# Strassen products for two blocks of the SwiGLU feed-forwards of a two-layer trunk

## The chip, the core and the metric

The kernel runs on one core of a Trainium2 chip, as one program. The metric is the device time in microseconds (us) of one execution, taken as the median of several runs. All arithmetic is float32; TensorE gets its precision from operands split in two (below).

## The reference, cut to what matters

Two layers. Each layer is a SwiGLU feed-forward (FFN) with half weight, a token mixer, and a second such FFN. There are 256 tokens of width 1024; the hidden width of an FFN is 2816. The four FFNs are what the change touches:

```
def _rms_norm(x, g):
    y = x32 * lax.rsqrt(jnp.mean(x32 * x32, axis=-1, keepdims=True) + EPS)
    return (y * g.astype(jnp.float32)).astype(x.dtype)

def _swiglu(h, w_gate, w_up, w_down):
    return (jax.nn.silu(h @ w_gate) * (h @ w_up)) @ w_down

x = x + 0.5 * _swiglu(_rms_norm(x, ffn1_norm[l]), ffn1_w_gate[l], ffn1_w_up[l], ffn1_w_down[l])
...   # mixer: input projection, causal convolution, latent attention, gates, output projection
x = x + 0.5 * _swiglu(_rms_norm(x, ffn2_norm[l]), ffn2_w_gate[l], ffn2_w_up[l], ffn2_w_down[l])
```

Here h is [256, 1024], w_gate and w_up are [1024, 2816], w_down is [2816, 1024].

## The kernel before, in words

**Products.** Every operand of TensorE is kept as a rounded part (whi, hThi, gThi) and the remainder (wlo, hTlo, gTlo). One float32 product is three matmuls (`products`, L663 to L665): hi by hi, hi by lo, lo by hi.

**Units.** Weights pass through the core in units of [128 partitions, 2048] float32, 1 MB each. SyncE (SP) loads a unit by two DMAs of 512 KB into `raw` (3 buffers); ScalarE (ACT) rounds it into `whi` (`split`, L1123); VectorE (DVE) subtracts to get `wlo` (`split`, L1517). whi and wlo have RING = 6 slots, so a unit can be made only after TensorE (PE) has released the unit six places before it. Each raw buffer comes free when the wlo of the unit three places before is done. All of these are one numbered sequence, and each engine's program is a list written out by hand in which the order of the work is fixed.

**The FFN.** The 2816 features go in 11 chunks c of 256 columns. A chunk has two units G0, G1 (gate and up columns of the upper and of the lower half of the 1024 rows) and one unit D (256 rows of w_down). For a tile of 128 tokens (t = 0, 1), `gate_up(c, t)` sums 8 x 3 matmuls of 512 columns into one PSUM bank; `down(c, t)` does 4 x 3 matmuls of 512 columns. So a chunk is 72 matmuls of 512 columns, and PE runs gate_up(c, 0), gate_up(c, 1), down(c-2, 0), down(c-2, 1) (`pair`). Between them ACT takes the silu (L1216), DVE multiplies (`mul`, L1623), ACT separates the halves of the words (`split_planes`, L1225), SP turns them by a transposing DMA (`plane_turn`), DVE joins them (`join`, L1636), ACT rounds (`round_joined`, L1233) and DVE subtracts (`rest_joined`, L1522). The chunks in the middle run in hardware loops on each engine, two to a turn.

**Around it.** At the start of an FFN two units are ready; the ring fills up while PE works on the first chunks. GpSimd (POOL) does one `root` (L531) for each RMS norm, and once in each layer a chain of some 70 small operations for the rotary angles (L549 to L588), which in the program stands right after the root of the first FFN; ACT waits for its end at the start of the mixer, and the roots of the mixer's norm stand behind it in POOL's program. In the mixer POOL also subtracts 12 units in each layer (L645).

Of the kernel before, what the change touches and what calls it, by code (L numbers as in the profile page):

```python
# [26 lines left out]
P = 128  # L27
# [29 lines left out]
U_FFN = 3 * NCH  # L57
# [4 lines left out]
assert U_LAYER % RING == 0 and U_LAYER % RAW == 0  # L62
# [32 lines left out]
def unit_gu(f, c, h):  # L95

    if isinstance(c, int) and c < 2:
        return UB[f] + 2 * c + h
    return c * 3 + (UB[f] - 2 + h)

def unit_down(f, c):

    if isinstance(c, int) and c >= NCH - 2:
        return UB[f] + U_FFN - NCH + c
    return c * 3 + (UB[f] + 6)
# [21 lines left out]
def trunk(nc, a):  # L128
    with ExitStack() as ctx:
# [16 lines left out]
        gain = sb("gain", [P, D])  # L146
        gates = sb("gates", [P, TT, 2 * D])
        ktok = sb("ktok", [P, TT, H, QK])
        vtok = sb("vtok", [P, TT, H, VD])
        cu = sb("cu", [P, CT, W - 1 + SEQ])  # L150
        cacc = sb("cacc", [P, CT, SEQ])
        qkT = sb("qkT", [P, 2, 2 * SEQ])
        pT = sb("pT", [P, 2, 3 * P])
        bias = sb("bias", [P, C])
# [14 lines left out]

        ss = small[:, 0:2]  # L170
# [12 lines left out]
        g_turned = vtok[:, 0, :, :].rearrange("p h d -> p (h d)")  # L183
# [3 lines left out]
        spare = ktok.rearrange("p t h d -> p (t h d)")  # L187
        block_words = (qkT[:, 0, :], spare[:, 0:512])
        block_turned = (turned, spare[:, 512:1024].bitcast(U16).rearrange("p (j r) -> p j r", r=P))
        block_out = (g_turned, cacc[:, 0:2, :].rearrange("p c n -> p (c n)"))  # L190
        sgate = gates[:, 0, 0:TT * FC].rearrange("p (t f) -> p t f", t=TT)
        gu = gates[:, 1, 0:TT * FC].rearrange("p (t f) -> p t f", t=TT)
# [115 lines left out]
        stored = sem("stored")  # L308

# [6 lines left out]
        def unit_waits(eng, l, u):  # L316

            eng.wait_ge(wlo_ready, l * U_LAYER + u + (RAW + 1))
# [4 lines left out]

        def per_ffn(l, f, c, t):
            return l * (4 * NCH) + c * TT + (2 * NCH * f + t + 1)

# [24 lines left out]
        def gu_bank(c, t):  # L351

            return bank[:, (6 if isinstance(c, int) and c == 1 else 4) + t, :]

        def slot(u, n):
            return u % n
# [10 lines left out]

        block = ctx.enter_context(nc.Block())

        @block.sync
        def _(sp):
            def place(l, u, u0, pairs):

                sp.wait_ge(wlo_ready, l * U_LAYER + u + 1)
                for dst, src in pairs:
                    sp.dma_start(dst, src).then_inc(raw_landed[slot(u0, RAW)], 16)

            def gate_up(l, f, c, c0, h):
                u0 = unit_gu(f, c0, h)  # L380
                dst = raw[:, slot(u0, RAW), 0:2048].rearrange("p (k g n) -> p k g n", k=4, g=2)
                rows = slice(4 * h * P, 4 * (h + 1) * P)
                cols = bass.ds(c * FC, FC)
                place(l, unit_gu(f, c, h), u0, [
# [1618 lines left out]
```

## Time and profile before

| | |
|---|---|
| median of 3 runs | 1047.74 us (1047.26 to 1047.82) |
| the profiled execution, first to last instruction (span) | 1045.7 us |
| outside the span (median less span) | 2.0 us |
| PE busy | 1040.6 us |
| DVE busy | 687.1 us (66%) |
| ACT busy | 593.7 us (57%) |
| POOL busy | 248.9 us (24%) |
| DMA | 208.81 MB, queue of SP 63.6% of 16 engines' span |

A page of the profile gives for each engine its busy time, the granted clock of TensorE, the chain of work that ended last, and groups of instructions by source line. Matmuls overlap in the records: one of 512 columns is shown as 0.39 us, and what it costs is the distance from one start to the next. An engine's idle time is put down to whatever released it.

### The profile page before, as it was taken

To read this page: it belongs to the slowest core of one execution; us is meant where nothing else is said; L and a number is where in the kernel's file an instruction comes from. 1 tells how busy PE (TensorE), PEld (TensorE's weight loads), DVE (VectorE), ACT (ScalarE), POOL (GpSimd) and SP (SyncE) were. 2 spreads that over 40 slices of the span, in tenths; PEclk is the share of its full clock that TensorE was granted. 3 is DMA by queue.
4 is the path that set the end of the run, shared out by engine and by line. 5 is a ranking of instruction groups with operands and counts; after the bars stand their busy time and mean duration, and the time that the engine had idled before them with its cause. 6 is when DMAs were issued, how large, how long until landed. Compare 5 with 4: busy or idle time off the path is not lost.

```text
span 1045.7 us, 13767 instructions
## 1 busy us (share of the span) xinstructions
PE 1040.6 (100%) x5001; PEld 872.2 (83%) x5001; DVE 687.1 (66%) x911; ACT 593.7 (57%) x792; POOL 248.9 (24%) x258
## 2 busy tenths in 40 slices
PE   9999999999999999999999999999999999999998
PEld 6888888998888888888888888889988888888887
DVE  6755655698976766555576555656999677656551
ACT  6754544576874665445466454536778557645440
POOL 2960000148850000000048300002588300000000
PEclk9999999999999999999999999999999999999999
DMA  8977666455644696675569667565366366976641
GB/s 280 310 237 234 186 211 200 143 200 172 210 163 125 206 313 188 206 232 196 153 191 282 216 206 228 184 199 172 122 212 224 118 191 222 261 221 186 207 139 41
DMA packets 191555, 208.81 MB, mean 200 GB/s; under 512 B 64112, under 2 KB 162704, under 8 KB 191504
## 3 DMA queue, kind: packets, MB, share of 16 engines
q1 hardware_dynamic: 190288, 206.03, 63.6%
q10 hardware_dynamic: 1216, 2.11, 0.7%
q8 instruction: 31, 0.51, 0.2%
q14 instruction: 20, 0.16, 0.1%
HBM read 192.90 MB, written 1.05 MB: 185 GB/s over the span
## 4 chain that ended last, share of the span: by engine, by line
PE 98%; ACT 1%; DVE 1%; issue 0%; POOL 0%; ACTq 0%
PE bank L663 31%; PE bank L665 31%; PE bank L664 31%; PE bank L744 1%; PE bank L905 1%; PE bank L914 1%; PE bank L935 1%; PE bank L670 1%; PE bank L702 0%; PE bank L913 0%; PE bank L937 0%; DVE htok L1563 0%; DVE x L1611 0%; ACT htok L1132 0%; PE bank L923 0%; PE bank L963 0%
## 5 line engine op out<-in xcount | busy, mean ns | idle before, releaser
L1517 DVE TENSOR_TENSOR wlo<-raw,whi 128x2048 fp32r<-128x2048 f32 (+2 forms) x152 | 347.4, 2290 | 82.6 <-ACT whi L1123 81.5
L663 PE MATMUL bank<-whi,hThi 128*128 128x512 f32 (+1 forms) x976 | 378.4, 388 | 0.0
L665 PE MATMUL bank<-whi,hTlo 128*128 128x512 f32 (+1 forms) x976 | 373.7, 383 | 0.0
L664 PE MATMUL bank<-wlo,hThi 128*128 128x512 f32 (+1 forms) x976 | 373.6, 383 | 0.0
L1123 ACT ACTIVATE whi<-raw 128x2048 fp32r<-128x2048 f32 (+2 forms) x176 | 335.3, 1910 | 16.8 <-DMA raw<-in_ffn_w_up 7.3
L665 PEld LDWEIGHTS bank<-whi,hTlo 128*128 128x128 f32 x976 | 183.3, 188 | 35.7
L663 PEld LDWEIGHTS bank<-whi,hThi 128*128 128x128 f32 x976 | 183.4, 188 | 35.1 <-issue 0.3
L664 PEld LDWEIGHTS bank<-wlo,hThi 128*128 128x128 f32 x976 | 183.4, 188 | 34.8
L1216 ACT ACTIVATE gates<-bank,small 128x256 f32<-128x256 f32 x88 | 41.8, 475 | 263.5 <-PE bank L665 262.8
L663 PE MATMUL bank<-whi,gThi 128*128 128x512 f32 (+1 forms) x416 | 162.2, 390 | 0.0
L664 PE MATMUL bank<-wlo,gThi 128*128 128x512 f32 (+1 forms) x416 | 161.1, 387 | 0.0
L665 PE MATMUL bank<-whi,gTlo 128*128 128x512 f32 (+1 forms) x416 | 161.1, 387 | 0.0
L531 POOL TENSOR_TENSOR small<-small,expo 128x1 f32<-128x1 f32 (+3 forms) x20 | 24.2, 1214 | 566.3 <-DVE small L1556 529.5
L1623 DVE SCALAR_TENSOR_TENSOR gates<-bank,small,gates 128x256 f32<-128x256 f32 x88 | 42.4, 483 | 168.1 <-ACT gates L1216 168.0
L645 POOL TENSOR_TENSOR wlo<-raw,whi 128x2048 fp32r<-128x2048 f32 x24 | 110.2, 4612 | 21.9 <-ACT whi L1123 21.9
L1717 DVE SCALAR_TENSOR_TENSOR bank<-cu,vec,bank 128x256 f32<-128x256 f32 x240 | 98.1, 479 | 0.2
L665 PEld LDWEIGHTS bank<-whi,gTlo 128*128 128x128 f32 x416 | 78.1, 188 | 16.0
L663 PEld LDWEIGHTS bank<-whi,gThi 128*128 128x128 f32 x416 | 78.1, 188 | 15.8 <-issue 0.4
L664 PEld LDWEIGHTS bank<-wlo,gThi 128*128 128x128 f32 x416 | 78.2, 188 | 15.5
L1225 ACT ACTIVATE qkT<-gates 128x512 uint16<-128x512 uint16 x80 | 49.5, 620 | 0.0
L549 POOL TENSOR_TENSOR small<-expo 128x1 f32<-128x1 f32 x72 | 36.5, 507 | 5.9
L663 PE MATMUL bank<-hThi,whi 128*128 128x256 f32 x128 | 36.4, 284 | 0.0
(177 smaller groups left out, 823.6 us busy)
## 6 DMA issues: line engine op xcount, KB each, us to landing
raw<-in_ffn_w_down SPq DMA_DIRECT2D x88, 512.0 KB, 4.2
raw<-in_ffn_w_gate SPq DMA_DIRECT2D x84, 512.0 KB, 4.3
raw<-in_ffn_w_up SPq DMA_DIRECT2D x84, 512.0 KB, 5.4
raw<-in_w_in SPq DMA_DIRECT2D x48, 512.0 KB, 4.8
raw<-in_w_out SPq DMA_DIRECT2D x16, 512.0 KB, 4.4
raw<-in_w_in SPq DMA_DIRECT2D x8, 544.0 KB, 4.5
raw<-in_w_mla_out SPq DMA_DIRECT2D x8, 512.0 KB, 3.9
raw<-in_w_conv_out SPq DMA_DIRECT2D x8, 512.0 KB, 4.7
```

The lines of the kernel that those rows point to most:

```text
L531: return nc.gpsimd.tensor_tensor(out, in_, expo[:, :].to_broadcast([P, out.shape[-1]]), ALU.pow)
L549: nc.gpsimd.tensor_tensor(small[:, 95:96], expo[:, :], expo[:, :], ALU.mult)
L645: nc.gpsimd.tensor_tensor(wlo[:, slot(u, RING), 0:n], raw[:, slot(u, RAW), 0:n], whi[:, slot(u, RING), 0:n].bitcast(F32), ALU.subtract).th ...
L663: nc.tensor.matmul(out, lh, rh, start=start, stop=False, skip_group_check=skip)
L664: nc.tensor.matmul(out, lh, rl, start=False, stop=False, skip_group_check=skip)
L665: return nc.tensor.matmul(out, ll, rh, start=False, stop=stop, skip_group_check=skip)
L1123: nc.scalar.activation(whi[:, slot(u0, RING), 0:USED[u0]], raw[:, slot(u0, RAW), 0:USED[u0]], ACT.Copy).then_inc(whi_ready, 1)
L1216: nc.scalar.activation(sgate[:, t, :], gu_bank(c, t)[:, 0:FC], ACT.Silu, scale=rs[:, t:t + 1]).then_inc(silu_ready, 1)
L1225: nc.scalar.activation(planes[:, :, :, t, :], words, ACT.Copy).then_inc(planes_ready, 1)
L1517: nc.vector.tensor_tensor(wlo[:, slot(u0, RING), 0:n], raw[:, slot(u0, RAW), 0:n], whi[:, slot(u0, RING), 0:n].bitcast(F32), ALU.subtract) ...
L1623: nc.vector.scalar_tensor_tensor(out=gu[:, t, :], in0=gu_bank(c, t)[:, FC:2 * FC], scalar=rs[:, t:t + 1], in1=sgate[:, t, :], op0=ALU.mult ...
L1717: ins = nc.vector.scalar_tensor_tensor(out=o, in0=i, scalar=w, in1=o, op0=ALU.mult, op1=ALU.add)
```

## The change

Chunks 3 and 4, and chunks 7 and 8 (features 768 to 1279 and 1792 to 2303), are computed as two blocks of 512 features. A block's input product has 2 x 2 x 2 quarters: token tiles t, halves of the 1024 rows, gate or up columns. Before, that is 8 quarter products of 4 x 3 matmuls. The change does 7, by Strassen's scheme in Winograd's form:

- On the weights, four sums of quarters (B11 is the upper quarter of gate, B21 its lower one, B22 the lower quarter of up): T1 = B11 + upper quarter of up, T2 = T1 + B22, T3 = both quarters of up, T4 = T2 + B21; the signs are in the sums of the tokens. The new list of units for a block is B11, T1, D, T2, B22, B21, T3, T4, D: nine units, where the two chunks had six. T1 and T2 are added by DVE into `chain[0]`; T3 and T4 are made by DMAs of GpSimd that add the lower quarter from HBM into `chain[1]` and `chain[0]` (`add_rows`, two DMAs of 512 KB each). chain[0] lies in `htok`, chain[1] in the memory of ktok and pT.
- On the tokens, once for an FFN: h is put together again (`whole_rows`), four sums of quarters (`mixed_rows`), rounded (`mixed_round`) and subtracted (`mixed_rest`) into new tiles sThi, sTlo. These share their memory with gain, bias, vtok and cu.
- On the results: PE leaves some products in the same bank and goes on adding to them; ACT copies the bank in between (`keep`, four a block), DVE adds or subtracts the copies (`up_first`, `gate_first`, `up_second`, `gate_second`), ACT's silu and DVE's multiply then work on 512 columns at once.

All engines' loops are written out, in a new order; an FFN has 39 units instead of 33. POOL's `sums` (the four `add_rows` of an FFN) stands in its program after the roots of that FFN's norm, and in the first FFN of a layer before the rotary angles. The memset of cu moves into the mixer. The core of the diff:

```
-U_FFN = 3 * NCH
+BLK = (3, 7)
+CW = 2 * FC
+PRODUCTS = ("B11", "T1", "D0", "T2", "B22", "B21", "T3", "T4", "D1")
...
             for l in range(DEPTH):
                 norm(l, 0)
+                sums(l, 0)
...
+            def add_rows(l, f, c, name):
+                done = per_block(l, f, c)
+                if name == "T3":
+                    pool.wait_ge(chain_landed[1], done * 32)
+                    pool.wait_ge(sum_ready["T1"], done)
+                    dst, src = chain[1], quarter_of(wu[f], l, c, 1)
+                if name == "T4":
+                    pool.wait_ge(wlo_ready, l * U_LAYER + unit_block(f, c, "T2") + 1)
+                    dst, src = chain[0], quarter_of(wg[f], l, c, 1)
+                dst = dst.rearrange("p (k n) -> p k n", k=4)
+                for k in (0, 2):
+                    nc.gpsimd.dma_start(dst[:, k:k + 2, :], src[:, k:k + 2, :],
+                                        accum_op=ALU.add).then_inc(sum_ready[name], 16)
...
+                    block_product(c, "B11", 4, plain_T(0, 0))
...
+                    block_product(c, "T1", 5, mixed_T(1, 1))
+                    down(c - 2, 0)
+                    down(c - 2, 1)
+                    pe.wait_ge(kept_ready, (done - 1) * 4 + 1)
+                    block_product(c, "T2", 4, mixed_T(0, 0), start=False)
+                    pe.wait_ge(kept_ready, (done - 1) * 4 + 2)
+                    block_product(c, "B22", 5, mixed_T(1, 0), start=False)
+                    pe.wait_ge(gu_ready, per_gu(l, f, at6, 0))
+                    block_product(c, "B21", 6, plain_T(1, 0))
+                    pe.wait_ge(kept_ready, (done - 1) * 4 + 3)
+                    block_product(c, "T3", 4, mixed_T(0, 1), start=False)
+                    pe.wait_ge(gu_ready, per_gu(l, f, at6, 1))
+                    block_product(c, "T4", 7, plain_T(1, 1))
+                    down(c - 1, 0)
+                    down(c - 1, 1)
...
                 first()
-                pair(2, 2)
-                pair(3, 3)
-                with pe.Fori(0, (NCH - 5) // 2) as i:
-                    pair(i * 2 + 4, 4)
-                    pair(i * 2 + 5, 5)
+                pair(2)
+                strassen(3)
+                pair(5)
+                pair(6)
+                strassen(7)
+                pair(9)
                 last()
```

DVE's list of one FFN, up to the end of the first block (the second block's follows the same pattern):

```
+                    gate_split(1, 0)
+                    gate_split(1, 1)
                     mul(0, 0)
                     norm_scale(l, 2 * f, 1)
+                whole_rows()
+                if (l, f) != (0, 0):
+                    mul(0, 1)
+                mixed_rows()
+                gate_split(2, 0)
+                gate_split(2, 1)
+                down_split(0)
+                join(0)
+                mul(1, 0)
+                mul(1, 1)
+                of_chain(3, "B11")
+                add_T1(3)
+                rest_joined(0)
+                mixed_rest()
+                mul(2, 0)
+                mul(2, 1)
+                of_chain(3, "T1")
+                join(1)
+                add_T2(3)
+                down_split(1)
+                rest_joined(1)
+                of_chain(3, "T2")
+                lower(3, "B22")
+                lower(3, "B21")
+                of_chain(3, "T3")
+                join(2)
+                up_first(3)
+                rest_joined(2)
+                of_chain(3, "T4")
+                down_split(2)
+                up_second(3)
+                gate_first(3)
+                block_mul(3, 0)
+                gate_second(3)
+                gate_split(5, 0)
+                block_mul(3, 1)
+                gate_split(5, 1)
```

ACT's list around the third to fifth product of the first block:

```
+                sum_of(3, "T2")
+                keep(3, 0, "B11")
+                lower(3, "B22")
+                lower(3, "B21")
+                split_planes(2, 1)
+                keep(3, 1, "T1")
+                sum_of(3, "T3")
+                keep(3, 2, "T2")
+                round_joined(2)
+                sum_of(3, "T4")
+                down_split(2)
+                keep(3, 3, "T3")
```

## Rows read from the trace of the kernel before

**Rows 1.** The page: span, busy time of the engines, TensorE's granted clock.

```profile
span 1045.7 us, 13767 instructions
...
PE 1040.6 (100%) x5001; PEld 872.2 (83%) x5001; DVE 687.1 (66%) x911; ACT 593.7 (57%) x792; POOL 248.9 (24%) x258
...
PEclk9999999999999999999999999999999999999999
```

**Rows 2.** The page: the chain that ended last, share of the span by engine.

```profile
PE 98%; ACT 1%; DVE 1%; issue 0%; POOL 0%; ACTq 0%
```

**Rows 3.** Timeline of PE in an FFN: start us, us, what.

```profile
60.03 0.39 PE L664 MATMUL bank<-wlo,gThi 128*128 128x512 f32 x1
...
65.25 0.39 PE L663 MATMUL bank<-whi,hThi 128*128 128x512 f32 x1
```

**Rows 4.** Groups by line and shape: busy us, mean ns | idle before, releaser.

```profile
L1517 DVE TENSOR_TENSOR wlo<-raw,whi 128x2048 fp32r<-128x2048 f32 x146 | 334.4, 2294 | 79.6 <-ACT whi L1123 78.5
L1123 ACT ACTIVATE whi<-raw 128x2048 fp32r<-128x2048 f32 x170 | 324.5, 1913 | 16.1 <-DMA raw<-in_ffn_w_up 7.3 <-DMA raw<-in_w_in 4.6 <-DMA raw<-in_ffn_w_down 1.6
...
L1636 DVE COPY vtok<-qkT 128x1024 uint16<-128x1024 uint16 x40 | 30.2, 755 | 0.0
L1522 DVE TENSOR_TENSOR gTlo<-vtok,gThi 128x512 fp32r<-128x512 f32 x40 | 27.4, 686 | 3.3 <-ACT gThi L1233 3.3
L1233 ACT ACTIVATE gThi<-vtok 128x512 fp32r<-128x512 f32 x40 | 24.9, 622 | 18.1 <-DVE vtok L1636 17.6 <-PE bank L665 0.5
```

**Rows 5.** A stretch of one chunk: length, busy (x) of PE, PEld, DVE, ACT, POOL, PEclk, DMA share, GB/s.

```profile
395.00:411.30 16.30, 16.30 (x74) 13.50 (x73) 9.12 (x7) 7.92 (x8) 0.00 (x0) 1.00 0.68 210
```

**Rows 6.** Timeline at the start of the second FFN: PE, ACT, DVE.

```profile
345.07 0.39 PE L663 MATMUL bank<-whi,hThi 128*128 128x512 f32 x1
...
347.79 1.03 PE L702 MATMUL bank<-ident,x 128*128 128x128 f32 x8
...
350.44 1.97 ACT L1123 ACTIVATE whi<-raw 128x2048 fp32r<-128x2048 f32 x1
352.25 0.52 ACT L1216 ACTIVATE gates<-bank,small 128x256 f32<-128x256 f32 x1
...
352.44 2.29 DVE L1517 TENSOR_TENSOR wlo<-raw,whi 128x2048 fp32r<-128x2048 f32 x1 [0.67 <-ACT whi L1123]
354.65 0.48 DVE L1623 SCALAR_TENSOR_TENSOR gates<-bank,small,gates 128x256 f32<-128x256 f32 x1
```

**Rows 7.** The first FFN: DVE before the unit G0 of chunk 2, and PE.

```profile
24.73 0.87 DVE L1623 SCALAR_TENSOR_TENSOR gates<-bank,small,gates 128x256 f32<-128x256 f32 x2
25.57 2.29 DVE L1517 TENSOR_TENSOR wlo<-raw,whi 128x2048 fp32r<-128x2048 f32 x1
...
32.62 0.38 PE bank L663
```

**Rows 8.** Loads of units: KB and median us to landing, then all of SP's.

```profile
raw<-in_ffn_w_up SPq DMA_DIRECT2D x84, 512.0 KB, 5.4
...
DMA to landing us min/median/max: 3.1/4.7/9.5
```

**Rows 9.** Rotary angles on POOL, the root behind them; DVE beside them; stretch of each layer's.

```profile
22.29 0.19 POOL L554 CAST small<-posi 128x2 f32<-128x2 int32 x1
...
36.27 0.20 POOL L549 TENSOR_TENSOR small<-expo 128x1 f32<-128x1 f32 x1
36.54 2.44 POOL L564 TENSOR_SCALAR ang<-ang 128x32 f32<-128x32 f32 x1
...
179.89 0.57 POOL L531 TENSOR_TENSOR small<-small,expo 128x1 f32<-128x1 f32 x1 [107.03 <-DVE small L1556]
...
36.53 2.29 DVE L1517 TENSOR_TENSOR wlo<-raw,whi 128x2048 fp32r<-128x2048 f32 x1 [0.29 <-ACT whi L1123]
...
22.30:72.90 50.60, 50.60 (x224) 41.72 (x223) 35.91 (x29) 32.39 (x34) 45.53 (x88) 1.00 1.00 293
536.70:587.30 50.60, 50.60 (x225) 41.92 (x224) 34.05 (x25) 29.86 (x31) 45.33 (x88) 1.00 0.94 283
```

More of the change, by code:

```diff
@@ L61 @@
 UM = U_FFN
-assert U_LAYER % RING == 0 and U_LAYER % RAW == 0
+assert U_LAYER % RING == 0
+LOADED = [u for f in range(2) for u in range(UB[f], UB[f] + U_FFN)
+          if FFN_UNITS[u - UB[f]][0] in ("G0", "G1", "D", "B22", "B21")] + list(range(UM, UM + U_MIX))
+LOADED.sort()
+R_LAYER = len(LOADED)
+UPPER = (1, 5, 9)
+SUM = {"T1": 1, "T2": 1, "T3": 32, "T4": 32}
+PLAIN = [c for c in range(NCH) if not any(b <= c < b + 2 for b in BLK)]
 M_PR, M_C01, M_UQ, M_UKV, M_C23, M_G, M_MLA, M_CO, M_WO = 0, 2, 4, 5, 6, 8, 16, 18, 20
@@ new lines, in ffn @@
+                down(l, f, 4)
+                turn(4)
+                chain_load(l, f, 7, 1)
+                down(l, f, 5)
+                turn(5)
+                lower_load(l, f, 7, "B22")
+                lower_load(l, f, 7, "B21")
+                turn(6)
+                down(l, f, 6)
+                gate_up(l, f, 9, 0)
+                gate_up(l, f, 9, 1)
+                down(l, f, 7)
+                gate_up(l, f, 10, 0)
+                turn(7)
+                gate_up(l, f, 10, 1)
@@ L808, in turn, with down @@
                     ins.then_inc(gtr, 1)
-                def down(c, c0, t, last=False, between=None):
+                def down(c, t, last=False, between=None):
                     pe.wait_ge(glo, per_ffn(l, f, c, t))
@@ new lines, in ffn @@
+                split_planes(5, 1)
+                round_joined(4)
+                first_of(7, "B11")
+                silu(6, 0)
+                sum_of(7, "T1")
+                silu(6, 1)
+                down_split(5)
+                round_joined(5)
+                split_planes(6, 0)
+                split_planes(6, 1)
+                sum_of(7, "T2")
+                round_joined(6)
+                lower(7, "B22")
+                keep(7, 0, "B11")
+                lower(7, "B21")
+                keep(7, 1, "T1")
@@ new lines, in ffn @@
+                gate_split(5, 0)
+                block_mul(3, 1)
+                gate_split(5, 1)
+                join(3)
+                down_split(3)
+                rest_joined(3)
+                gate_split(6, 0)
+                join(4)
+                mul(5, 0)
+                gate_split(6, 1)
+                mul(5, 1)
+                down_split(4)
+                of_chain(7, "B11")
+                rest_joined(4)
+                add_T1(7)
+                mul(6, 0)
+                join(5)
@@ new lines, in ffn @@
+                of_chain(7, "T1")
+                mul(6, 1)
+                add_T2(7)
+                down_split(5)
+                rest_joined(5)
+                of_chain(7, "T2")
+                join(6)
+                lower(7, "B22")
+                rest_joined(6)
+                lower(7, "B21")
+                of_chain(7, "T3")
+                of_chain(7, "T4")
+                down_split(6)
+                up_first(7)
+                gate_split(9, 0)
+                up_second(7)
```

593 lines of the change are left out of this document (442 added, 151 removed).

## The prediction

> **What bounds the kernel now.** I read the page first: of a span of 1045.7 us PE is busy 1040.6, at the full granted clock (2.4 GHz) in every slice [rows 1]. DVE and ACT are at 66% and 57% [rows 1]. The chain that ended last is PE to 98% [rows 2]. So the bound is the number of matmuls, and a matmul taken away is worth its whole distance to the next, provided that nothing else becomes late. In the timeline of an FFN the reader should look at starts, not at durations: from 60.03 to 65.25 there are 23 matmuls of 512 columns, 0.227 us each [rows 3]. A chunk of 72 is 16.3 us. In one such stretch DVE is busy 9.1 us and ACT 7.9, with the DMA engines at 0.68 [rows 5]: the room that the added work has to fit in.
>
> **What is removed.** Two chunks take 96 matmuls for gate and up; a block takes 7 x 12 = 84. That is 12 less for each block, 96 for eight blocks (two in each of four FFNs): 96 x 0.227 = 21.8 us, all of it on the path. This term I trust most. 1047.7 - 21.8 = 1025.9 is the floor; I see nothing by which it could go lower, since PE had no gaps that the written-out loops could close.
>
> **What is added on PE.** No matmul. More waits, at each product instead of at each second one; each costs only if what is waited for is late. So the rest is a question of lateness, for DVE, ACT, the adding DMAs and POOL.
>
> **DVE and ACT, in sum.** For a block: nine units instead of six (3 more remainders of 2.29 us, 3 more roundings of 1.91 [rows 4]), two sums T1 and T2 (an operation of three operands of the same size as a remainder, so 2.29 each), four sums of results and two multiplies of 512 columns (0.69 each, as L1522 [rows 4]), four copies on ACT (0.62 each, as L1233 [rows 4]). DVE in a block: 9 x 2.29 + 2 x 2.29 + 6 x 0.69 + two joins (0.76) and two rests (0.69) = 32.2 us; PE takes 132 x 0.227 = 29.9 us. So DVE is slower than PE inside a block, and it fits only by what was made ahead in the six slots and by the light chunks between. For an FFN: whole_rows, mixed_rows and mixed_rest add 2.29 + 4 x 0.69 + 2.29 = 7.3 us, at its start, where the ring is only two units deep.
>
> **DVE, step by step in the first block.** Take PE's times in units of 12 matmuls, 2.72 us: in the second FFN they start at 345.07, and eight transposes at 347.79 put in some 0.85 [rows 6], so product number k starts at 345.9 + 2.72 k. G0 of chunk 2 is due at k = 8 (367.7), D0 at k = 12 (378.6), T4 at k = 22 (405.8), G0 and G1 of chunk 5 at k = 25, 26 (413.9, 416.6). Queued remainders follow each other at 2.21 us and roundings at 1.81, small DVE operations at 0.4 to 0.65 (354.65 less 352.44, 352.25 less 350.44 [rows 6]). Walking DVE's list from 352.44: two remainders to 356.9; mul, scale, whole_rows, mul to 360.0; mixed_rows with its waits for its own steps to 362.7; G0 of chunk 2 ready at 364.9, slack 2.8; G1 3.0; D0 ready 369.6; join, two muls, B11 373.2, T1's sum 375.4, rest_joined(0) 376.0, slack 2.6 to D0's product; mixed_rest 378.2; mul(2,1) waits for PE (378.6) and silu to 379.5; T1 381.7, slack 5; join, T2's sum 384.5, D1 386.7, rest_joined(1) 387.3, slack 2.1; T2 389.5; B22, B21, T3 to 396.1. Then `up_first` waits at the head of DVE's queue until PE has done B22 (k = 20, 400.3), and rest_joined(2), T4, D2 and the units of chunk 5 stand behind it: T4 403.8, slack 2.0; D2 406.0, slack 2.5; after the four sums and a multiply G0 of chunk 5 at 412.1, slack 1.8, and G1 at 414.9, slack 1.7. So no product is late, but everything has only some 2 us, and a list of 40 steps has handoffs of about 0.1 us that I left out. The second block begins with a full ring, and the same walk gives 3.5 us and more. I put 0.2 us a block for handoffs, 1.6 us in all; bounds 0 and, if each first block loses what its slack falls short of a 2 us error, 4 x 2 = 8.
>
> **The first FFN** has no slack to begin with. DVE is done with its two muls at 25.57 and then made G0 of chunk 2, which PE took at 32.62 [rows 7]. Now whole_rows and mixed_rows (2.2 + 2.7) come before it: 25.6 + 4.9 + 2.3 = 32.8. That is 2.9 us less slack than in the other FFNs, and so at rest_joined(1) about 0.8 us late. Cost 1.0 us; bounds 0 and 3, since the DMA engines are at 1.00 in that stretch [rows 9].
>
> **The adding DMAs.** The trace of before has none. T3's can start at 375.4 and is wanted by ACT at some 392, so it is covered. T4's may be issued only when T2's remainder is done (389.5), since it changes chain[0] in place; ACT would take it at 398.6. Behind it on ACT stand D2's rounding, `keep` of T3 and the units of chunk 5. With DVE's 1 us of reserve there and the slack of 1.7, PE loses nothing while the two DMAs land within L = 11.8 us of T2's remainder. In the second block T2' can't be ready before PE has ended gate_up(6, 1) (k = 35, 441.1), then silu, mul, sum, D5, rest and remainder, 449.2; T4' is due at k = 45 (468.3), less 1.9 and 2.3: L may be 14.9. A plain load of half a unit lands in 4.7 us in the median, 5.4 for w_up, at most 9.5 [rows 8]. Lower bound of L: 4.7. Upper bound: an add reads two sources, twice the slowest, 19. The nearest is twice the 5.4, 10.8, with an issue of two DMAs ahead of it: about 11.5, just inside. Price of L: 4 (L - 11.8) + 4 (L - 14.9), so nothing at 11.5 and 45 us at 19. A page of the Trainium skill speaks to this: "Collectives: The Full Stack", "The bandwidth ceiling", says that a reducing transfer is half as fast as a copy because the add needs two source reads. With the fixed 2.0 us plus bytes / 436e3 of "DMA: Bandwidth & Descriptors", "Anatomy of one DMA", an estimate from the two is 2.0 + 2 x 2.4 = 6.8 us for 1 MB, and the cost of T4 would be 0. No run here shows either so far. Of bytes: 2 MB more for each block, 16 to 208.8 MB; at a share of 0.68 this has room outside the first 60 us.
>
> **POOL's queue.** In the first FFN of each layer the rotary angles now stand behind `sums`, and so behind the wait for T2' of the second block. They take 50.6 us in both layers [rows 9] (ends 72.9 and 587.3). In the first FFN product k starts at 32.6 - 8 x 2.72 = 10.9 plus 2.72 k; T2' is ready 8.3 us after k = 35, at 114.4, the issues take some 2 us, the angles end at 167. The root behind them ran at 179.89 [rows 9], and is due 5.4 us earlier now (two blocks less), at 174.5: 7.5 us to spare, so cost 0. ACT's wait for the angles comes later still. What they could lose: POOL's small operations grow from 0.2 to 2.44 us when a remainder of DVE runs (36.54 beside 36.53 [rows 9]). DVE's load beside them was 35.9 and 34.1 of 50.6 us [rows 9]; in the new place I count 13 remainders and some small ones, 34 of 53, the same.
>
> **Sum.** 1047.7 - 21.8 + 1.6 + 1.0 = 1028.5 us. The profiled execution would be at 1026.5 by its own span (2.0 outside it).
>
> **The rivals.**
> 1. *The adding DMAs are late* (L = 12 to 16): PE waits before T4 of the first block of each FFN, then of the second as well. For it: they compete with D2's and chunk 5's loads, the slowest plain landing is 9.5, and POOL makes two of them. Against: the DMA share of 0.68. At L = 14, 4 x 2.2 = 9 us: 1037. Chance 0.15.
> 2. *The angles are late.* If the denser DVE stretches them by a quarter, to 63 us, they end at 180, 5 us behind the root's due time in two layers, which PE has some 2 us of cover for: 6 us, up to 12 if more: 1035 to 1041. By the page "SBUF — State Buffer", "Who interferes with whom", a DVE operation with two inputs in SBUF contends with GpSimd's reads; by that rule the row pair at 36.5 agrees, and the stretch grows with DVE's count in that time. Chance 0.10.
> 3. *DVE is late in the first block* by handoffs that my walk lacks, 1 to 3 us in each FFN: 1031 to 1038. Chance 0.09.
> 4. *Slower than before.* The one mechanism is again the landing of T4, now as a rate: if an add moves float32 so slowly that 8 L - 106.8 exceeds the gain of 19.2 (what is left after the two terms above), so from L = 15.8 us on, less than 67 GB/s for the megabyte. At the bound of 19 it is 1028.5 + 45 = 1074. Chance 0.06.
> 5. *It doesn't save what it says*, because products with waits at each 12 matmuls leave gaps of about 0.2 us in PE: 7 waits x 8 x 0.2 = 11 us, 1040. Against: PE waited as often in the mixer with no gap in its busy time. Chance 0.03.
>
> **How the numbers follow.** The forecast (every lateness under about 4 us in sum, 1026 to 1031) has 0.57. Rivals 1, 2, 3 and 5 together 0.37, nearly all faster still, since they give 1031 to 1044. Rival 4 has 0.06. The range: down to 1025.4, the floor less the spread of the runs; up to 1039, which takes in rivals 3, most of 1 and half of 2; above it I leave some 0.13. A measurement can tell about 0.2% (2.1 us) from no change: faster means under 1045.6, same 1045.6 to 1049.8. From the cases: faster 0.91, same 0.03, slower 0.06.
>
> **What the profile after would show.** 96 fewer matmuls of 512 columns, 4905 in all, and PE's sum of gaps under 9 us. If the forecast holds, PE has no idle time named after whi or wlo outside the first 60 us; the adds land within 12 us; the last rotary operation ends by 170 and by 680. Wrong if: PE idles before T4 (k = 22) in each FFN, released by DVE after ACT after a DMA (rivals 1 and 4); idles at the start of the mixer, with POOL's root behind the angles (rival 2); idles a little before many products of the first block with DVE never idle (rival 3); or shows small gaps at every wait (rival 5).

## The result: slower by 4%

The changed kernel takes 1089.87 us (median of 4 runs, 1082.84 to 1093.68), the kernel before, beside it, 1047.50 (1046.66 to 1047.82). The ratio is 1.040, 95% interval 1.0383 to 1.0417. The forecast was 1028.5 us, in a range of 1025.4 to 1039, with 0.06 for slower: wrong in size and in sign. The profiled execution has a span of 1087.0 us and took 1088.85.

The page of the changed kernel, to be held against [rows 1]:

```profile
span 1087.0 us, 13335 instructions
...
PE 1037.7 (95%) x4905; PEld 864.5 (80%) x4905; DVE 811.7 (75%) x992; ACT 661.2 (61%) x836; POOL 288.7 (27%) x290
...
PEclk9989998999999998999999899999999999989999
...
q0 software_dynamic: 8704, 16.78, 9.6%
```

The 96 matmuls are gone (4905), yet PE is busy for 1037.7 us, only 2.9 less than before. It is idle for 49.3 us, where it was idle for 5.1. And its granted clock is not full in every slice any more (the line PEclk, in tenths). The last line of the view is the queue of GpSimd's adding DMAs: packets, MB, and their share of the 16 DMA engines' time. PE's list of waits (what it waited for; us in total, times, longest) names two places:

```profile
PE bank L854 <- DVE wlo L1880: 33.3, 9, 6.0
PE bank L1053 <- DVE gates L1989: 10.5, 4, 4.3
```

The first is the product T4, once in each of the eight blocks (in order of time 5.98, 2.53, 4.94, 1.41, 4.68, 4.69, 5.58 and 3.32 us) and once for 0.2 us, before G0 of chunk 2 in the first FFN. The second is the last chunk's turn at the end of each FFN (4.29, 2.68, 2.56, 1.01), which the prediction did not look at.

With the 96 x 0.227 = 21.8 us that were to go, the span adds up: 1045.7 - 21.8, plus 44.2 more idle time (49.3 - 5.1), plus 18.9 of PE's busy time over 1040.6 - 21.8 = 1018.8, gives 1087.0.

**T4's add, in one block.** Timeline of the changed kernel, first block of the second FFN: start us, us, what (and the idle time before it):

```profile
400.20 2.28 DVE L1880 TENSOR_TENSOR wlo<-htok,whi 128x2048 fp32r<-128x2048 f32 x1
...
402.85 1.21 POOL L717 DMA_DIRECT2D htok<-in_ffn_w_gate  x1 [5.83 <-DVE wlo L1880]
409.06 1.52 POOL L717 DMA_DIRECT2D htok<-in_ffn_w_gate  x1 [5.01 <-issue]
...
419.16 1.91 ACT L1369 ACTIVATE whi<-htok 128x2048 fp32r<-128x2048 f32 x1 [7.56 <-DMA htok<-in_ffn_w_gate]
...
421.11 2.29 DVE L1880 TENSOR_TENSOR wlo<-htok,whi 128x2048 fp32r<-128x2048 f32 x1 [6.61 <-ACT whi L1369]
...
423.55 0.76 PE L854 MATMUL bank<-whi,hThi 128*128 128x512 f32 x1 [4.94 <-DVE wlo L1880]
424.11 0.63 PE L855 MATMUL bank<-wlo,hThi 128*128 128x512 f32 x1
...
428.37 0.58 PE L856 MATMUL bank<-whi,hTlo 128*128 128x512 f32 x1
428.79 0.39 PE L854 MATMUL bank<-whi,gThi 128*128 128x512 f32 x1
```

T2's remainder is done at 402.48 and POOL issues the first add 0.37 us later. The second add leaves only at 409.06, 6.2 us behind the first, though POOL has nothing else to do ("issue" as the releaser: the profile shows nothing it waited for). ACT gets the sum at 419.16. So L, counted from the end of T2's remainder to ACT's start, is 16.7 us, and PE is 4.94 us late. Four stretches of the same time show the DMA engines before the landing and TensorE after its wait (length; busy of PE, PEld, DVE, ACT, POOL; granted clock; DMA share; GB/s):

```profile
402.90:409.00 6.10, 6.10 (x29) 5.05 (x28) 6.10 (x3) 3.72 (x4) 1.16 (x1) 1.00 0.95 211
409.10:419.10 10.00, 9.51 (x42) 7.53 (x41) 2.05 (x3) 1.12 (x2) 1.48 (x1) 1.00 0.95 259
...
423.50:428.80 5.30, 5.25 (x13) 4.13 (x14) 4.05 (x4) 3.56 (x3) 0.00 (x0) 0.50 0.83 271
428.80:434.00 5.20, 5.20 (x24) 4.31 (x23) 5.01 (x4) 3.29 (x5) 0.00 (x0) 1.00 0.49 155
```

The DMA share is 0.95, not the 0.68 of [rows 5]. And after the wait the granted clock is 0.50, the lower of the two levels (1.2 GHz): behind the first of them the matmuls of T4 stand 0.427 us apart, where the following ones are 0.23 apart. A wait of 4.94 us thus costs about another 12 x 0.2 = 2.4 us, which is booked as busy. Over the whole trace 72 distances are so wide, in eight runs of 7 to 11 (14 single ones in the mixers are not counted: the kernel before has them too). The eight runs stand behind or soon after the waits of 2.56, 3.32, 4.29, 4.68, 4.69, 4.94, 5.58 and 5.98 us; behind the waits of 1.01, 1.41, 2.53 and 2.68 us there are none. That is 72 x 0.2 = 14.4 of the 18.9 us. The length of a wait does not decide it alone: in the kernel of experiment 2 eight wide distances follow a wait of 2.03 us, and none follow one of 3.19 us.

**The end of an FFN.** SP, ACT, DVE and PE at the end of the second FFN:

```profile
516.85 0.38 SPq L485 DMA_DIRECT2D raw<-in_ffn_w_gate  x1
...
517.88 1.63 SPq L534 DMA_TRANSPOSE qkT<-qkT  x1
...
510.95 1.15 ACT L1522 ACTIVATE qkT<-gates 128x512 uint16<-128x512 uint16 x2 [0.88 <-DVE gates L1989]
512.60 3.71 ACT L1369 ACTIVATE whi<-raw 128x2048 fp32r<-128x2048 f32 x2
...
514.53 6.76 DVE L1880 TENSOR_TENSOR wlo<-raw,whi 128x2048 fp32r<-128x2048 f32 x3 [1.04 <-ACT whi L1369]
523.14 0.74 DVE L2004 COPY gates<-qkT 128x1024 uint16<-128x1024 uint16 x1 [1.85 <-DMA qkT<-qkT]
...
525.84 0.44 PE L1053 MATMUL bank<-ident,gates 128*128 128x128 f32 x2 [2.68 <-DVE gates L1989]
```

Chunk 9's planes are ready at 512.1, but its transpose is issued at 517.88: in SP's program it stands behind the load of the next unit, and that one waits until a raw buffer is free, at 516.8 (the first of DVE's three remainders from 514.53). The join at 523.14, the rounding, the multiply of chunk 10 and PE follow from there.

SP's order is the same in the kernel before, where it cost nothing. There the load had left at 492.23 and the planes were ready at 495.84, so that the transpose left at 495.86:

```profile
492.23 0.38 SPq L377 DMA_DIRECT2D raw<-in_ffn_w_gate  x1
...
495.86 1.23 SPq L402 DMA_TRANSPOSE qkT<-qkT  x1
...
495.22 0.62 ACT L1225 ACTIVATE qkT<-gates 128x512 uint16<-128x512 uint16 x1
```

What the change moved is the moment at which the raw buffer comes free. The load waits for the remainder of D8. ACT's list before had the rounding of D8 ahead of chunk 9's planes; the new list has it behind them and behind chunk 8's rounding (`split_planes(9, 1)`, `round_joined(8)`, `down_split(8)`), where it starts at 512.60 without a wait. That this place in ACT's list alone frees the buffer late is read from the lists and the trace; no run moved it back.

### The profile page after: what moved, and what is told of

Read it like the earlier page. It is cut to its first block and busy times, and to the rows that moved or that the text cites. A ratio compares the mean times of both kernels' runs of the same rounds, so it can differ in the third digit from the quotient of the medians.

```text
span 1087.0 us, 13335 instructions
## 1 busy us (share of the span) xinstructions
PE 1037.7 (95%) x4905; PEld 864.5 (80%) x4905; DVE 811.7 (75%) x992; ACT 661.2 (61%) x836; POOL 288.7 (27%) x290
## 3 DMA queue, kind: packets, MB, share of 16 engines
q0 software_dynamic: 8704, 16.78, 9.6%
## 5 line engine op out<-in xcount | busy, mean ns | idle before, releaser
L854 PE MATMUL bank<-whi,hThi 128*128 128x512 f32 (+1 forms) x816 | 321.8, 394 | 33.3 <-DVE wlo L1880 33.3
L1880 DVE TENSOR_TENSOR wlo<-raw,whi 128x2048 fp32r<-128x2048 f32 (+2 forms) x136 | 308.1, 2284 | 32.0 <-ACT whi L1369 31.9
L856 PE MATMUL bank<-whi,hTlo 128*128 128x512 f32 (+1 forms) x816 | 316.1, 387 | 0.0
L855 PE MATMUL bank<-wlo,hThi 128*128 128x512 f32 (+1 forms) x816 | 316.1, 387 | 0.0
L1369 ACT ACTIVATE whi<-raw 128x2048 fp32r<-128x2048 f32 (+2 forms) x160 | 301.5, 1907 | 14.9 <-DMA raw<-in_w_in 4.4
L854 PEld LDWEIGHTS bank<-whi,hThi 128*128 128x128 f32 x816 | 156.1, 191 | 66.1 <-issue 36.8
L1880 DVE TENSOR_TENSOR wlo<-htok,whi 128x2048 fp32r<-128x2048 f32 x32 | 73.2, 2288 | 62.4 <-ACT whi L1369 62.4
L1369 ACT ACTIVATE whi<-htok 128x2048 fp32r<-128x2048 f32 x32 | 61.3, 1915 | 87.3 <-DMA htok<-in_ffn_w_gate 54.0
L717 POOL DMA_DIRECT2D heads<-in_ffn_w_up x16 | 19.8, 1239 | 311.5 <-DVE htok L2028 270.8
L2246 DVE SCALAR_TENSOR_TENSOR bank<-shared,vec,bank 128x256 f32<-128x256 f32 x240 | 98.1, 479 | 0.2
L854 PEld LDWEIGHTS bank<-whi,gThi 128*128 128x128 f32 x416 | 79.6, 191 | 16.9 <-issue 0.7
L1522 ACT ACTIVATE qkT<-gates 128x512 uint16<-128x512 uint16 x80 | 48.3, 623 | 42.3 <-DMA qkT<-qkT 17.4
L2004 DVE COPY gates<-qkT 128x1024 uint16<-128x1024 uint16 x40 | 30.2, 754 | 38.6 <-DMA qkT<-qkT 38.6
```

Of the source, the lines that this page charges most:

```text
L717: nc.gpsimd.dma_start(dst[:, k:k + 2, :], src[:, k:k + 2, :], accum_op=ALU.add).then_inc(sum_ready[name], 16)
L854: nc.tensor.matmul(out, lh, rh, start=start, stop=False, skip_group_check=skip)
L855: nc.tensor.matmul(out, lh, rl, start=False, stop=False, skip_group_check=skip)
L856: return nc.tensor.matmul(out, ll, rh, start=False, stop=stop, skip_group_check=skip)
L1369: nc.scalar.activation(whi[:, slot(u, RING), 0:USED[u]], src, ACT.Copy).then_inc(whi_ready, 1)
L1522: nc.scalar.activation(planes[:, :, :, t, :], words, ACT.Copy).then_inc(planes_ready, 1)
```

## The experiments

Kernel N below is the kernel of experiment N. Ratios are to the kernel before, run beside it.

**1. T4's add left out.** The T4 adds and ACT's wait for them go; everything else stays. T4's product then takes T2's sum, so the values are not the right ones.

```
-                add_rows(l, f, 3, "T4")
...
-                add_rows(l, f, 7, "T4")
...
+                    if name != "T4":
+                        act.wait_ge(sum_ready[name], per_block(l, f, c) * SUM[name])
```

> This kernel leaves out the adding DMAs of T4 (8 of 16 pairs) and ACT's wait for them, so the T4 product uses T2's sum; all else stands. Theory A (the landing of T4's add, 14 to 17 us behind T2's remainder, makes PE wait, and the clock's fall after each wait comes with it): the eight waits of PE before the T4 product (33.3 us in all) go, about 2.5 us of half clock behind each go too, so 1089.9 - 33 - 8 x 2.4 = some 1038 if the waits at turn(10, 0) stay (10.5 us), some 1026 to 1030 if they go as well. Rival B (DVE itself is late in the first block, the add only comes last): PE waits 2 to 4 us at other products of the same blocks, 1045 or more.

Measured: 1039.11 us (1038.29 to 1039.93), ratio 0.992 (0.9903 to 0.9943). That is 1 us from the 1038 expected for the case that the waits at the FFN's end stay. PE's waits inside the blocks are gone; those at the FFN's end are 7.4 us. So T4's add is worth some 50 us, and the Strassen order alone is faster than before.

**2. Plain copies in place of the adds.** The same queue, bytes, places and waits, without the accumulation (the sums then hold other values):

```
-                    nc.gpsimd.dma_start(dst[:, k:k + 2, :], src[:, k:k + 2, :],
-                                        accum_op=ALU.add).then_inc(sum_ready[name], 16)
+                    nc.gpsimd.dma_start(dst[:, k:k + 2, :], src[:, k:k + 2, :]).then_inc(sum_ready[name], 16)
```

> This kernel makes the four GpSimd DMAs of an FFN plain copies (no add), with the same waits, so the chains hold other values. If reading two sources makes the adds slow (the rule that a reducing transfer goes at half the rate): the second DMA of a pair is issued some 3 us behind the first instead of 6.2, and the time falls to about 1050. If GpSimd's way of issuing is what is slow, whatever the operation: the distance stays at 5 to 6.2 us and the time stays over 1075.

Measured: 1037.61 us (1036.39 to 1038.82), ratio 0.991 (0.9889 to 0.9929): even less than the 1050 expected. From its page (span, PE, the queue) and POOL's timeline:

```profile
span 1034.6 us, 13335 instructions
...
PE 1021.5 (99%) x4905; PEld 854.8 (83%) x4905; DVE 811.5 (78%) x992; ACT 658.6 (64%) x836; POOL 288.4 (28%) x290
...
q0 software_dynamic: 4608, 16.78, 4.9%
...
388.90 1.45 POOL L717 DMA_DIRECT2D htok<-in_ffn_w_gate  x2 [11.80 <-DVE wlo L1879]
```

Both copies are issued within 1.45 us, and no product waits. The same 16.78 MB take 4.9% of the engines' time in 4608 packets, as adds 9.6% of a longer span in 8704. So neither the bytes nor POOL's place is what is slow; the accumulation is, in two ways: about twice the engine time, and the second DMA held back. The whole difference to the changed kernel is 1087.0 - 1034.6 = 52.4 us: 33.1 of waits before T4, 3.0 at the FFN's ends, and 16.2 of PE's busy time, for the same 4905 matmuls. Kernel 2 has 8 wide distances, behind one wait at an FFN's end, where the changed kernel has 72: 64 x 0.2 = 12.8 of the 16.2 us is the lower clock.

The doubling agrees with the Trainium skill, "Collectives: The Full Stack", "The bandwidth ceiling: the fold count and why AG ≠ RS ≠ AR", where the reducing step of a collective needs two source reads; this case has no collective, so the agreement is in the factor alone. The prediction's estimate of 6.8 us for 1 MB, with the formula of the Trainium skill, "DMA: Bandwidth & Descriptors", "Anatomy of one DMA", is not borne out: 16.7 us here, for two DMAs one after the other beside the loads of another queue.

**3. Four adds of 256 KB in place of two of 512 KB.**

```
-                for k in (0, 2):
-                    nc.gpsimd.dma_start(dst[:, k:k + 2, :], src[:, k:k + 2, :],
+                for k in range(4):
+                    nc.gpsimd.dma_start(dst[:, k:k + 1, :], src[:, k:k + 1, :],
```

Measured: 1107.41 us (1104.57 to 1109.22), ratio 1.057 (1.0551 to 1.0592): worse. That two or three pieces go out at once was as expected, the gain was not. POOL's timeline, same block:

```profile
396.16 2.82 POOL L717 DMA_DIRECT2D heads<-in_ffn_w_up  x3 [16.75 <-DVE htok L2028]
404.48 0.87 POOL L717 DMA_DIRECT2D heads<-in_ffn_w_up  x1 [5.49 <-issue]
409.54 2.66 POOL L717 DMA_DIRECT2D htok<-in_ffn_w_gate  x3 [4.20 <-DVE wlo L1880]
422.54 0.87 POOL L717 DMA_DIRECT2D htok<-in_ffn_w_gate  x1 [10.35 <-issue]
```

Three small adds go out in a row; the fourth waits 5.5 us, for T4 10.35. So it is not that every add waits for the one before: in this block three of 256 KB go out, or one of 512 KB. The last piece starts later than the second half did, 13.0 us behind the first piece against 6.2, and L is 19.8 us (409.23 to 429.02) in place of 16.7; PE's waits for remainders grow to 50.7 us. That the room is one for packets fits the numbers but was not tried by itself: the queue's packets divided by its DMAs are 272 for an add of 512 KB, 144 for one of 256 KB and 144 for a copy of 512 KB, so what goes out together has 3 x 144 = 432, 272 or 2 x 144 = 288 packets, and two adds of 512 KB would have 544.

**4. The transpose ahead of the next load.** Only SP's order at the two places where a new stage begins:

```
                     else:
-                        gate_up(l, f, 0, 0)
                         if f == 0:
                             plane_turn(l - 1, 1, NCH - 2)
+                        gate_up(l, f, 0, 0)
...
-                    if h == 1:
+                    if h == 0:
                         plane_turn(l, 0, NCH - 2)
```

> Only the order of two steps in SP's list: the transposing DMA of chunk 9 ahead of the load of the unit behind the FFN, which waits for D8's remainder. Theory: in the changed kernel that wait holds the transposing DMA back by some 5 us (issued 517.9, planes ready some 512), and PE waits at turn(10, 0) for 10.5 us in all; so 8 to 11 us less, 1079 to 1082, with the waits before T4 as they were. Rival: the join is late since DVE is behind from the late T4s, and the order doesn't matter: 1088 to 1090.

Measured: 1076.69 us (1075.16 to 1080.60), ratio 1.029 (1.0254 to 1.0316). PE's waits at the turn fall from 10.5 to 1.4 us, its busy time from 1037.7 to 1034.8, while T4's waits are 34.4 instead of 33.3: 10.7 us between the spans, 13 between the medians, where 8 to 11 were expected. With T4's waits unchanged, the second place costs on its own; experiments 6 and 7 show 9.4 us for the same edit where T4's waits are gone.

**5. T3 and T4 added by GpSimd** from the raw buffer of B22 and B21, which are loaded anyway:

```
-                    nc.gpsimd.dma_start(dst[:, k:k + 2, :], src[:, k:k + 2, :],
-                                        accum_op=ALU.add).then_inc(sum_ready[name], 16)
+                nc.gpsimd.tensor_tensor(dst, dst, raw[:, raw_slot(l, u), 0:2048],
+                                        ALU.add).then_inc(sum_ready[name], 1)
```

SP also waits for these sums before it fills the two raw buffers again, here and wherever DVE makes a sum (experiments 6, 7 and 9 to 11), so that a buffer is held longer.

> T3 and T4 are added by GpSimd's TENSOR_TENSOR from the raw buffers of B22 and B21, which are loaded anyway, in place of the adding DMAs: 4.6 us each by the 24 remainders that GpSimd makes in the mixer. T4 is ready 5 us behind T2's remainder, where DMAs took 14 to 17. Theory A: PE's waits before T4 go, 1026 to 1040, faster than before. Rival B (DVE's list in the first block is the limit): 1045 or more. If GpSimd's reads beside DVE's slow DVE (two inputs from SBUF each), DVE's remainders would be shown longer than 2.29 us.

Measured: 1076.59 us (1075.32 to 1080.70), ratio 1.028 (1.0260 to 1.0294). The time misses the 1026 to 1040 expected: the waits moved to another product. POOL and DVE in its timeline:

```profile
388.28 4.95 POOL L719 TENSOR_TENSOR heads<-heads,raw 128x2048 f32<-128x2048 f32 x1 [16.31 <-DVE htok L2030]
406.29 11.63 POOL L719 TENSOR_TENSOR htok<-htok,raw 128x2048 f32<-128x2048 f32 x1 [13.06 <-DVE wlo L1882]
...
388.67 6.72 DVE L1889 TENSOR_TENSOR sTlo<-gates,sThi 128x2048 fp32r<-128x2048 f32 x1
...
406.13 4.48 DVE L1882 TENSOR_TENSOR wlo<-raw,whi 128x2048 fp32r<-128x2048 f32 x2
410.54 2.28 DVE L1882 TENSOR_TENSOR wlo<-heads,whi 128x2048 fp32r<-128x2048 f32 x1
```

A subtraction of DVE that takes 2.29 us elsewhere takes 6.72 beside POOL's add; POOL's next add takes 11.63 us while three remainders of DVE run through it undisturbed. The two do not share, they take turns, and whoever comes second waits. PE now waits for `rest_joined`'s output gTlo (17.6 us, eight times, 2.5 or less) where it waited for T4, and still 10.3 us at the FFN's ends. This agrees with the Trainium skill, "SBUF — State Buffer", "Who interferes with whom", which calls the port pair that the two share an exclusive lock; what the trace adds is that POOL's operation can be held over several of DVE's.

**6. T4 added by DVE**, from the raw buffer of B21; T3 stays an adding DMA:

```
+                def add_T4(c):
+                    split_of(c, "T2")
+                    add(c, "T4", lower_raw(c, "B21"))
...
                 join(2)
+                add_T4(3)
                 up_first(3)
...
                 lower(7, "B21")
+                add_T4(7)
                 of_chain(7, "T3")
```

> T4's sum by DVE from B21's raw buffer, T3's still by adding DMAs. DVE gets 2.2 us more in each block, of which it idled 2.75 us ahead of up_first in the first. Theory A (T4's landing): as without T4's add at all, 1036 to 1042, the waits at turn(10, 0) left. Rival B (DVE's list has no room): PE waits 1 to 3 us at D2 or G0 of chunk 5 in each FFN, 1045 to 1055.

Measured: 1042.51 us (1042.02 to 1044.77), ratio 0.996 (0.9947 to 0.9973). No product waits for T4 (waits for a remainder 0.8 us in all); the FFN's ends cost 8.7 us. It is just over the 1036 to 1042 expected.

**7. Both: T4 by DVE, and the transpose ahead of the load.**

> Both edits: T4 by DVE and the transposing DMA of chunk 9 first. If the two causes are all that is wrong: 1026 to 1031, the floor of 1025.9 nearly reached, and faster than before by some 1.8%. If there is a third: over 1034.

Measured: 1033.15 us (1030.69 to 1033.61), ratio 0.986 (0.9843 to 0.9879). PE is busy 1020.8 us of a span of 1031.0, with a granted clock of 1.0. The time lies between my two cases, 1026 to 1031 and over 1034: the two causes are nearly all, and 3.7 us of waits stay at the turn.

**8. T4's product after D's**, so that the add has 24 more matmuls (5.4 us) to land; the adds stay, the lists of ACT and DVE follow.

```
-                    pe.wait_ge(gu_ready, per_gu(l, f, at6, 1))
-                    block_product(c, "T4", 7, plain_T(1, 1))
                     down(c - 1, 0)
                     down(c - 1, 1)
+                    pe.wait_ge(gu_ready, per_gu(l, f, at6, 1))
+                    block_product(c, "T4", 7, plain_T(1, 1))
```

> The adding DMAs stay, but T4's product comes behind the 24 matmuls of D, 5.4 us later (with the lists of ACT and DVE to match). The add lands 14 to 17 us behind T2's remainder; PE then needs it by some 17 us in the first block. Theory A: waits before T4 shrink from 33 us in all to 0 to 8, 1045 to 1060 with the waits at turn(10, 0). If each microsecond of a wait costs only itself: near 1060. If the clock's fall behind a wait goes with it: below 1050.

Measured: 1085.35 us (1084.43 to 1090.79), ratio 1.038 (1.0342 to 1.0413), far over what I expected. PE's waits:

```profile
PE bank L1053 <- DVE gates L1989: 22.4, 4, 6.3
PE bank L854 <- DVE wlo L1880: 16.7, 16, 2.1
PE bank L854 <- DVE gTlo L1887: 3.4, 5, 0.8
```

The waits for remainders are halved and spread over 16 places, but the turn at the FFN's end now costs 22.4 us instead of 10.5. The adds leave as far apart as before (400.46 and 406.84). ACT still stands idle for T4's landing in each of the eight blocks, 45.6 us in all where it was 53.8 in the changed kernel, so room on PE did not free the engines that wait for the DMA in order. As I read it, what stands behind that wait in the lists of ACT and DVE comes late at another place. SP's order has a part in it that is open: at the end of the second FFN the transpose leaves 5.8 us behind its planes (508.24 to 514.02), as in the changed kernel, and this kernel was not run with the order of experiment 4.

**9. As 7, with silu and multiply of chunk 10 ahead of chunk 9's rounding and join.**

```
-                round_joined(c - 1)
                 silu(c, 0)
+                round_joined(c - 1)
...
+                mul(c, 0)
                 join(c - 1)
                 rest_joined(c - 1)
-                mul(c, 0)
```

> As the kernel with T4 by DVE and the transposing DMA of chunk 9 first, and at the end of an FFN silu(10, 0) and mul(10, 0) come ahead of chunk 9's rounding and join, since PE wants them first. If what is left of PE's waits at turn(10, 0) (3.7 us in four FFNs, with some 2 us of lower clock behind them) comes from that order: 1033.2 less 4 to 6, 1027 to 1029. If it comes from DVE being behind in its whole list: no change, 1033.

Measured: 1031.44 us (1030.24 to 1033.84), ratio 0.985 (0.9831 to 0.9868). The wait at the turn is gone, but 4.3 us of a new one stand one step on, before the product with chunk 9's remainder (gTlo). It can't be told from kernel 7 (1033.15), and misses the 1027 to 1029 I expected. It has the lowest median of the study, 1.5% under the kernel before.

**10. T3 by DVE, T4 by the adding DMA**: the mirror of kernel 6, to see whether T3's adds in POOL's queue are what holds T4's up.

```
+                def add_T3(c):
+                    dve.wait_ge(sum_ready["T1"], per_block(l, f, c))
+                    add(c, "T3", lower_raw(c, "B22"))
...
                 lower(3, "B22")
+                add_T3(3)
                 lower(3, "B21")
```

> The opposite choice: T3 by DVE, T4 still by the two adding DMAs, all else as in the changed kernel. If T4's lateness comes partly from T3's pair still being in the DMA queues and in GpSimd's: its add lands 2 to 3 us earlier, and the waits before T4 fall from 33 to 15 us or so, 1065 to 1075. If T4's own two DMAs, one behind the other, are all of it: 1085 to 1095, with DVE's 2.2 us more in each block.

Measured: 1077.81 us (1077.06 to 1078.57), ratio 1.029 (1.0271 to 1.0312). POOL, ACT and PE in the first block of the second FFN:

```profile
399.80 1.31 POOL L718 DMA_DIRECT2D htok<-in_ffn_w_gate  x1 [30.18 <-DVE wlo L1879]
406.15 1.23 POOL L718 DMA_DIRECT2D htok<-in_ffn_w_gate  x1 [5.03 <-issue]
...
416.30 1.91 ACT L1368 ACTIVATE whi<-htok 128x2048 fp32r<-128x2048 f32 x1 [6.68 <-DMA htok<-in_ffn_w_gate]
...
420.68 0.77 PE L853 MATMUL bank<-whi,hThi 128*128 128x512 f32 x1 [5.12 <-DVE wlo L1879]
```

POOL had been idle for 30 us, and still the second add leaves 6.35 us behind the first and L is 416.30 - 399.43 = 16.9 us. So in the first blocks it is T4's own pair. In the second blocks the four waits (11.9 us in the changed kernel) are gone, all but 0.2 us of the 20.3: there L is 12.5 to 12.6 us, against 13.8 to 17.4 in the changed kernel, so there T3's adds did hold T4's up. In the changed kernel's trace the first T4 add of three of the four second blocks has "issue" as what it waited for, as T3's second add has before it. The time, 1077.81, lies between my two cases, as each holds for half of the blocks.

**11. Both sums by DVE, no adding DMA, with the orders of 9.**

> Both sums by DVE and no adding DMA at all, with the two other edits of order. If T3's adding DMAs cost nothing since they are covered, DVE's 2.2 us more in each block cost 0 to 2 us in each first block: 1027 to 1037, not better than T4 alone by DVE. If they disturb the other transfers (transposes of 5.3 us in place of 3.0): 2 to 4 us better than T4 alone.

Measured: 1045.64 us (1044.31 to 1047.72, 10 runs), ratio 0.9985 (0.9976 to 0.9995): 14 us slower than kernel 9 for one more operation of 2.2 us in each block. DVE and PE in the second block of the second FFN:

```profile
462.04 2.29 DVE L2028 TENSOR_TENSOR heads<-heads,raw 128x2048 f32<-128x2048 f32 x1
464.25 2.28 DVE L1880 TENSOR_TENSOR wlo<-raw,whi 128x2048 fp32r<-128x2048 f32 x1
466.45 2.29 DVE L2028 TENSOR_TENSOR htok<-htok,raw 128x2048 f32<-128x2048 f32 x1
468.65 2.28 DVE L1880 TENSOR_TENSOR wlo<-heads,whi 128x2048 fp32r<-128x2048 f32 x1
...
466.68 0.47 PE L854 MATMUL bank<-whi,hThi 128*128 128x512 f32 x1 [0.76 <-DVE wlo L1880]
...
471.08 0.47 PE L854 MATMUL bank<-whi,sThi 128*128 128x512 f32 x1 [1.42 <-DVE wlo L1880]
```

Each sum stands ahead of the remainder of the next product, and PE waits for both remainders. The waits are 10.4 us for remainders and 4.4 for gTlo, and PE's busy time is 4.3 us over kernel 9's, at a granted clock of 1.0; where these 4.3 us lie is open. Of the two cases expected neither came. One of the two sums is worth giving to a DMA: T3's, which has the time.

## Why the prediction was wrong, by its own steps

**Matmuls removed: right.** 4905, at 0.227 us apart where nothing waits. Kernel 9 has PE busy for 1020.0 us, against 1018.8 worked out.

**DVE's walk of the first block: right.** It put T2's remainder at 389.5, 41.7 us behind the eight transposes at 347.79; in the changed kernel they stand at 360.44 and the remainder ends at 402.48, 42.0 behind, in the last FFN 43.3. T4's product was due at 405.8, 58.0 behind the transposes; PE came to it at 418.61, 58.2 behind. The term of 1.6 us for handoffs was not needed: kernels 1 and 2 show no wait in a block for a remainder. The first FFN cost 0.2 us and not 1.0. The walk of the second block was too short: in kernel 1, where nothing held it up, T2' remainder ended 105.2 us behind the transposes (347.47 to 452.64), not 449.2 - 347.8 = 101.4.

**T4's landing: the mechanism was right, the size wrong.** The step put L at 11.5, between 4.7 and 19, with nothing to pay up to 11.8. Measured, from T2's remainder to ACT's start, in the four first blocks: 16.2, 16.7, 16.4 and 16.1 us; in the four second blocks 14.5, 13.8, 17.4 and 16.1. The price of 4(L - 11.8) + 4(L - 14.9) at the two means, 16.4 and 15.5, is 18.4 + 2.4 = 20.8 us; measured were 21.2 in the first blocks and 11.9 in the second. In the block shown the formula holds to the digit, 16.7 - 11.8 = 4.9 for a wait of 4.94. The room (the landing less the wait) was right in two of the first blocks, 11.7 and 11.8, and 10.2 and 10.5 in those of the first and last FFN. In the second blocks it came out at 12.0 to 12.8 us, not at 14.9, as T2' remainder was later than walked. What made L itself too small:
- The doubled 5.4 us took the two DMAs of a unit as going side by side. They go one after the other, 6.2 us apart.
- The share of 0.68 came from one stretch of a plain chunk. Where T4's add runs, the share is 0.95, and the second DMA takes 10.1 us to land. The stretch that counts is the one in which the transfer will run, with what the change adds to it.

The nearest row was taken as the value although it lay 0.3 us inside the point where the cost begins; the bound of 19 was near the truth. With the price so steep (8 us for each us of L) and the row so far from an adding DMA, the chance of 0.21 for rivals 1 and 4 together was much too low. Rival 4 had the mechanism (from L = 15.8 us on slower than before, and the mean L was 15.9), though not what else the landing costs, which follows.

**PE after a wait: left out.** Every price of a wait was the wait alone. After 8 of the 10 waits of 2.5 us and more matmuls stand at the distance of the lower clock, 7 to 11 at a time, 14.4 us in sum. With waits of 1.2 us or less (kernel 9) PE's busy time is within 1.2 us of what was worked out. Rival 4's 8 L - 106.8 was therefore too cheap: at the mean L of 15.9 it gives 20.4 us; T4's adds cost 1087.0 - 1036.5 = 50.5 us of span (experiment 1).

**The end of the FFN: left out.** The prediction walked the first block and the start of the second, and of SP only the bytes. `plane_turn(9)` stands behind the load of the next stage's first unit, before and after; ACT's new list rounds D8 behind chunk 9's planes, so that this load now waits for its buffer when the planes are ready, and the transpose with it. 10.5 us of waits, 13 us in the median by experiment 4.

**The angles (rival 2): no cost, but nearer than the prediction had it.** They ran from 133.13 to 182.6, 49.5 us, and in the second layer from 668.97 to 716.84, so both missed the marks of 170 and 680. The root behind them still came at 192.20, after 9.6 us of idle time:

```profile
133.13 2.35 POOL L744 CAST small<-posi 128x2 f32<-128x2 int32 x1
...
182.39 0.20 POOL L739 TENSOR_TENSOR small<-expo 128x1 f32<-128x1 f32 x1
192.20 0.57 POOL L698 TENSOR_TENSOR small<-small,expo 128x1 f32<-128x1 f32 x1 [9.61 <-DVE small L1921]
```

The stretch itself was underrated. In kernel 1 they took 57 us in both layers, with 8.4 and 7.0 us to spare before the root. In kernel 9, where DVE makes T4's sums too, they took 61 us (115.43 to 176.60 and 623.19 to 684.85), close to rival 2's 63, and the root follows 1.3 and 0.3 us behind them, still released by DVE.

**Rival 5 (gaps at waits that are satisfied): not there.** Rival 3 (DVE late): not in the changed kernel; it appears when DVE gets both sums (experiment 11).

In sum: the profiled execution was put at 1026.5 and was 1087.0. Of the 60.5 us between, 33.3 are T4's waits, 10.5 the turn's, 18.9 PE's busy time over the sum, 0.4 small waits, less the 2.6 that were set aside for DVE.

## What to carry to other kernels

Put an adding DMA only where its result is wanted long after its source is ready (here 12.5 to 17.4 us for 1 MB): T3's adds were covered, T4's, the last link of a chain, were not, and one operation of 2.2 us on DVE replaced them. Where a change reorders an engine's list, walk the stage's end too, and the queue of the engine that issues the loads: a transfer that is ready may stand behind one whose buffer now comes free later. Price a wait of PE with the slower matmuls behind it, and give a cost that lies 0.3 us inside its threshold the chance of a coin.

## What the runs showed of the hardware that I had not expected

- An adding DMA from HBM of float32 takes about twice the engine time of a copy of the same bytes: 9.6% of 1087.0 us against 4.9% of 1034.6, in 8704 packets against 4608.
- Of the pairs of adds of 512 KB the second leaves 6.1 to 7.7 us behind the first; of four adds of 256 KB, in the block shown, three go out in 2.8 us and the fourth after 5.5 to 10.35 us of idle time. Two copies of 512 KB go out within 1.45 us. An add of 512 KB also holds POOL for 1.2 to 1.5 us, a copy for 0.7.
- After a wait of 4.94 us PE's granted clock was 0.50 and T4's matmuls were 0.427 us apart; in kernel 9, with waits of 1.2 us and less, no such run of wide distances is found.
- DVE and GpSimd, each with two operands in SBUF, take turns: 6.72 us instead of 2.29 on DVE, 11.63 instead of 4.6 on POOL, which was held over three operations of DVE.
